# VectorE's copies of a finished sequence's small results: from the front of a sample step to behind the second half of its selected scores

## The chip, the cores and the metric

The program runs on one core of one Trainium2 chip. A core has a TensorE (PE, with its weight load PEld), a VectorE (DVE), a ScalarE (ACT), a GpSimd (POOL) and a SyncE (SP) that here only issues transfers. Every engine runs its own instructions in their order; where one needs another's result it waits on a semaphore, and everything behind the waiting instruction on that engine waits with it. The metric is the device time of one execution in microseconds, the median of several runs.

## The reference

One layer of a decoder, run for a prompt of 512 tokens and for 8 sample sequences that share all weights. The part that matters here is the sample side: each of the 8 sequences has one new token and 4096 past positions. Cut to that:

```python
# per sample sequence b; SCALE and masks left out
o_s = softmax(q . k_selected) @ v_selected     # 15 selected blocks of 64 rows + the new row
o_w = softmax(q . k_window)   @ v_window       # the last 512 rows + the new row
o_mem = softmax(mq . k_mem)   @ v_mem          # 256 memory rows, 4 heads
o_fox = softmax(fq . k_past + decay) @ v_past  # all 32 pages of 128 rows
# prompt and sample: three branches, silu gates, and a merge
z = branch * silu(gate) @ w_branch
y = x + rmsnorm(sum_k sigmoid(xn @ w_gate_k) * z_k @ w_out, g_post)
```

## The kernel before

The kernel runs five stages one after the other: compression of cached pages, norms, the input projection, the prompt's attention, and `sample_and_merge`. The change lies in the last. It interleaves two jobs. The merge of the prompt is heavy matmul work, cut by `Plan` into items: a product is two gate halves of 260 columns (line 1730, x16 in the trace for one half) and, from the thirteenth product on, a branch product z (line 1738, x8 in the trace for one). The 8 sample sequences are 8 steps `b` of a loop that every engine walks in its own written order, with merge items in slots 0 to 8 of each step (`merge_until(b, slot)`), one or two items a slot. The last 3 sequences' fox attention (32 pages each of keys and values) is spread over the steps too.

What each engine does around the change, in step `b`:

- **VectorE** (the list in the diff below): selected scores of group 0 (`small_scores(b, "slc", 0)`, lines 2051 and 2055), merge slot 0, one group of page scores (`page_scores`, lines 2064 and 2066), then `small_sums(b - 1)`: it copies the previous sequence's small sums out of PSUM (lines 2138 and 2139). Behind it come `query_diagonal("nsa", b + 1)` (line 2027, the diagonal from which TensorE spreads the next query), the selected scores of group 1, merge slot 1, `place_sums(b - 2)` (line 2146), `query_diagonal("mem", b + 1)`, the window scores, the query rows (line 2033), memory scores (lines 2074 and 2076), more merge and page scores, and the maxima of the softmax (line 2099).
- **TensorE**: merge slot 0, `small_values(b - 1)` (lines 1803 and 1806, the previous sequence's weighted sums into PSUM), merge slot 1, `turn_sums(b - 2)` (line 1815), `spread_query("nsa", b + 1)` (line 1749), merge slot 2, `spread_query("mem", b + 1)`, merge slots 3 and 4 with `page_values` between (line 1766, fox values), then `softmax_step(b, 0)` (line 1777), which needs the maxima.

`small_sums(b - 1)` waits for two things: `small_free`, that `small_values(b - 1)` is done, and `sums_turned`, that `turn_sums(b - 2)` has read the one buffer `svs` it writes. On TensorE the second lies behind merge slot 1. TensorE's order in a step:

```python
merge_until(b, 0)
small_values(b - 1)          # -> small_free
merge_until(b, 1)
turn_sums(b - 2)             # -> sums_turned
spread_query("nsa", b + 1)   # waits for VectorE's diagonal
merge_until(b, 2)
spread_query("mem", b + 1)   # waits for VectorE's second diagonal
```

SyncE issues the transfers of pages in a fixed order (keys and values alternating): a key load waits for VectorE's `k_free` (line 1640 on), a value load for TensorE's `v_free` (line 1655), and each stands in line behind the ones before. There are three value buffers of two pages each. ScalarE turns the gate halves out of PSUM (line 1953 on) and loads the next gate weights. GpSimd gathers the selected rows two sequences ahead (line 1714).

Of the kernel before, what the change touches and what calls it, by code (L numbers as in the profile page):

```python
# [79 lines left out]
def after(engine, s, count):  # L80

    if count > 0:
        engine.wait_ge(s, count)
# [1438 lines left out]
def sample_and_merge(k):  # L1522
# [11 lines left out]
    with ExitStack() as cx:  # L1534
# [101 lines left out]
        with nc.Block() as block:  # L1636
# [354 lines left out]
            def _(ve):  # L1991
# [5 lines left out]
                def merge_product(product):  # L1997
                    ve.wait_ge(g_out, 2 * product + 2)
                    if product < SILU:
                        nc.vector.tensor_tensor(k.oT[:, product, :], e[product % 2], k.oT[:, product, :], ALU.mult).then_inc(e_free, 1)  # L2000
                        return
                    n = product - SILU
                    d, b = n // 3, n % 3
                    ve.wait_ge(z_done, n + 1)
                    if b == 2:
                        ve.wait_ge(mt_done, 2 * d + 1)
                    elif b == 1:
                        after(ve, mt_done, 2 * d)
                    nc.vector.scalar_tensor_tensor(out=tmp if b else mt[:, d, :], in0=e[product % 2], scalar=1.0, in1=z_bank[:, :],
                                                   op0=ALU.add, op1=ALU.mult).then_inc(e_free, 1)  # L2010
                    if b:
                        ve.wait_ge(e_free, product + 1)
                        nc.vector.tensor_tensor(mt[:, d, :], mt[:, d, :], tmp, ALU.add).then_inc(mt_done, 1)

                def merge_until(b, slot):

                    for product in range(merged[0], Plan.products(Plan.until(b, slot))):
                        merge_product(product)
                    merged[0] = max(merged[0], Plan.products(Plan.until(b, slot)))
# [4 lines left out]
                def query_diagonal(kind, b):  # L2024
                    after(ve, q_spread, event[kind, b])
                    q, seq = (k.qf, fox_at[b]) if kind == "fox" else (k.mq if kind == "mem" else k.qn, b)
                    nc.vector.tensor_tensor(qdiag, k.ident.unsqueeze(1).to_broadcast([P, 4, P]),  # L2027
                                            q[:, seq, :].unsqueeze(2).to_broadcast([P, 4, P]), ALU.mult).then_inc(qdiag_done, 1)
# [6 lines left out]
                def small_scores(b, kind, g):  # L2035

                    n, ss = b * 4 + parts_of(b).index((kind, g)), ss_of[b % 2]
                    ve.wait_ge(q_in, event["nsa", b] + 1)
                    after(ve, small_free, b - 1)
                    if kind == "win":  # L2040
                        ve.wait_ge(win_in, (b + 1) * 16)
                    else:
                        ve.wait_ge(slc_in[b % 2], (b // 2 + 1) * 16 * NSLC)
                    after(ve, small_scored, n - 1)
                    tiles = NWIN if kind == "win" else 8
                    feats = slice(g * HD, (g + 1) * HD)
                    keys = win[:, :, feats] if kind == "win" else slc[:, b % 2, g * 8:g * 8 + 8, feats]
                    at = (n % 2) * 2048
                    product = scratch[:, at:at + R * tiles * HD].rearrange("p (r n d) -> p r n d", r=R, n=tiles)
                    rows = qrows_of["nsa"][:, g * R * HD:(g + 1) * R * HD].rearrange("p (r d) -> p r d", r=R)  # L2050
                    nc.vector.tensor_tensor(product, keys.unsqueeze(1).to_broadcast([P, R, tiles, HD]),  # L2051
                                            rows.unsqueeze(2).to_broadcast([P, R, tiles, HD]), ALU.mult).then_inc(small_times, 1)
                    ve.wait_ge(small_times, n + 1)
                    first = ST if kind == "win" else 0
                    nc.vector.tensor_reduce(ss[:, first:first + tiles, g * R:(g + 1) * R].rearrange("p n r -> p r n"), product,  # L2055
                                            AX, ALU.add).then_inc(small_scored, 1)

                def page_scores(m):
                    b, g = EARLY + m // GROUPS, m % GROUPS
                    ve.wait_ge(k_in[m % KG], 16 * KR * (m // KG + 1))  # L2060
                    if g == 0:
                        ve.wait_ge(q_in, event["fox", first_step(b)] + 1)
                    pages = kpage[:, (m % KG) * KR:(m % KG + 1) * KR, :]
                    nc.vector.tensor_tensor(pages, pages, qrow[:, 0, :].unsqueeze(1).to_broadcast([P, KR, BRW]), ALU.mult).then_inc(k_times, 1)  # L2064
                    ve.wait_ge(k_times, m + 1)
                    nc.vector.tensor_reduce(k.pfe[:, b - EARLY, g * KR:(g + 1) * KR, :], pages.rearrange("p n (h d) -> p n h d", h=H),  # L2066
                                            AX, ALU.add).then_inc(k_free, 1)
# [67 lines left out]
                def small_sums(b):  # L2135
                    ve.wait_ge(small_free, b + 1)
                    after(ve, sums_turned, b)
                    nc.vector.tensor_copy(svs, sv_bank.rearrange("p (i n) -> p i n", i=2)).then_inc(os_out, 1)
                    nc.vector.tensor_copy(k.om[:, :, b:b + 1], om_turned.unsqueeze(2)).then_inc(os_out, 1)
# [42 lines left out]
                for b in range(NB):  # L2182
                    late = list(groups_of(b))
                    if b:
                        small_scores(b, "slc", 0)
                    merge_until(b, 0)
                    for m in late[0:1]:
                        page_scores(m)
                    if b:
                        small_sums(b - 1)  # L2190
                    if b < LASTB:
                        query_diagonal("nsa", b + 1)
                    if b:
                        small_scores(b, "slc", 1)
                    merge_until(b, 1)
                    if b > 1:
                        place_sums(b - 2)
                    if b - 1 in sums_after:
                        place_fox(sums_after[b - 1])
                    if b < LASTB:  # L2200
                        query_diagonal("mem", b + 1)
                    small_scores(b, "win", 0)
                    small_scores(b, "win", 1)
                    if b and b < LASTB:
                        query_row("nsa", b + 1)
                    merge_until(b, 2)
                    memory_scores(b)
                    if b and b < LASTB:
                        query_row("mem", b + 1)
                    merge_until(b, 3)  # L2210
                    for m in late[1:2]:
                        page_scores(m)
                    if b == 0:
                        small_scores(b, "slc", 0)
                        merge_until(b, 4)
                        small_scores(b, "slc", 1)
                        query_row("nsa", b + 1)
                        query_row("mem", b + 1)
                    merge_until(b, 4)
                    scores(b)  # L2220
                    softmax_max(b)
                    for m in late[2:3]:
                        page_scores(m)
                    merge_until(b, 5)
                    softmax_spread(b)
                    for m in late[3:4]:
                        page_scores(m)
                    if b + 1 in fox_at:
                        query_diagonal("fox", b + 1)
                    softmax_shift(b)  # L2230
                    merge_until(b, 6)
                    softmax_sum(b)
                    merge_until(b, 7)
                    softmax_norm(b)
                    if b + 1 in fox_at:
                        query_row("fox", b + 1)
                    if b in sums_after:
                        page_sums(sums_after[b])
                    if b in fox_of:
                        probabilities()  # L2240
                    merge_until(b, 8)
# [188 lines left out]
```

## Time and profile before

| what | value |
|---|---|
| median of 3 runs | 1405.1 us (1399.25 to 1415.84) |
| profiled execution | 1402.47 us, its span 1400.7 us |
| PE busy, share of the span | 1231.3 us, 88% |
| DVE busy, share of the span | 804.9 us, 57% |
| ACT, POOL busy | 229.1 us, 176.3 us |
| sample stage: first query to last `small_values` | 801 to 1316 us of the span |

The stage of interest is the last 600 us. Steps 1 to 7 begin on TensorE near 897, 952, 1013, 1074, 1136, 1199 and 1253 us (the `small_values` of the sequence before), and the eighth `small_values` is at 1312 us. In the timeline a row gives start, duration, engine, line, operation, tiles and shape, and in brackets the engine's idle time before it and what ended that. "cst" at line 2027 is the diagonal, and `d_ybuf` at line 2138 is the buffer `svs`. `score_banks` and `bank` are PSUM.

### The profile page before, as it was taken

To read this page: it belongs to the slowest core of one execution; us is meant where nothing else is said; L and a number is where in the kernel's file an instruction comes from. 1 tells how busy PE (TensorE), PEld (TensorE's weight loads), DVE (VectorE), ACT (ScalarE), POOL (GpSimd) and SP (SyncE) were. 2 spreads that over 40 slices of the span, in tenths; PEclk is the share of its full clock that TensorE was granted. 3 is DMA by queue.
4 is the path that set the end of the run, shared out by engine and by line. 5 is a ranking of instruction groups with operands and counts; after the bars stand their busy time and mean duration, and the time that the engine had idled before them with its cause. 6 is when DMAs were issued, how large, how long until landed. Compare 5 with 4: busy or idle time off the path is not lost. (4 is left out here: it accounts for less than half of the span.)

```text
span 1400.7 us, 23870 instructions
## 1 busy us (share of the span) xinstructions
PE 1231.3 (88%) x8308; PEld 841.1 (60%) x8308; DVE 804.9 (57%) x1168; ACT 229.1 (16%) x694; POOL 176.3 (13%) x150
## 2 busy tenths in 40 slices
PE   0889969999999569999999797988799898999996
PEld 0889958887888355444434476866556464665542
DVE  3445240798999862344544547577875868634123
ACT  0100141112111202233333400110000000000023
POOL 1010000200000000000000172244051331400000
PEclk9998989999999665999999988999999999999998
DMA  8899632577888502575876194566577776757620
GB/s 243 236 284 264 203 117 64 165 232 247 285 295 306 138 1 76 181 271 181 272 248 225 40 299 143 163 183 220 157 246 243 237 264 211 235 176 272 248 84 31
DMA packets 238846, 279.65 MB, mean 200 GB/s; under 512 B 21685, under 2 KB 159438, under 8 KB 238470
## 3 DMA queue, kind: packets, MB, share of 16 engines
q1 hardware_dynamic: 126534, 200.28, 42.9%
q10 hardware_dynamic: 105760, 60.01, 15.4%
q0 software_dynamic: 6432, 17.83, 3.9%
q8 instruction: 66, 1.08, 0.3%
q14 instruction: 54, 0.44, 0.1%
HBM read 271.13 MB, written 11.11 MB: 201 GB/s over the span
## 5 line engine op out<-in xcount | busy, mean ns | idle before, releaser
L1730 PE MATMUL bank<-xnT,e_wg 128*128 128x260 f32 x1152 | 280.1, 402 | 0.0
L1730 PEld LDWEIGHTS bank<-xnT,e_wg 128*128 128x128 f32 x1152 | 228.7, 201 | 53.4 <-issue 16.2
L580 PE MATMUL score_banks<-xnT,oT 128*128 128x260 f32 (+1 forms) x864 | 197.9, 387 | 7.5 <-DMA oT<-in_w_in 7.5
L1714 POOL DMA_INDIRECT d_slc<-in_cache_nsa_slc,selrow x128 | 153.6, 1200 | 274.6 <-PE score_banks L1806 235.2
L580 PEld LDWEIGHTS score_banks<-xnT,oT 128*128 128x128 f32 (+1 forms) x864 | 162.1, 190 | 37.8 <-DMA oT<-in_w_in 7.8
L253 PE MATMUL score_banks<-c_cols,c_w 128*64 128x128 f32 (+2 forms) x2304 | 121.3, 269 | 46.7 <-DVE c_cols L293 46.5
L253 PEld LDWEIGHTS score_banks<-c_cols,c_w 128*64 128x64 f32 x2304 | 119.5, 141 | 47.4 <-issue 47.1
L293 DVE COPY c_cols<-oT 128x1024 f32<-128x1024 f32 x48 | 49.8, 1163 | 87.1 <-DMA oT<-in_cache_nsa_cmp 80.4
L1393 DVE TENSOR_REDUCE f_pt<-score_banks 128x2 f32<-128x512 f32 (+3 forms) x56 | 45.1, 805 | 80.5 <-PE score_banks L1314 78.4
L1738 PE MATMUL bank<-oT,e_wb 128*128 128x512 f32 x192 | 90.7, 617 | 0.0
L1358 PE MATMUL bank<-mt,rpast 128*8 128x512 f32 x320 | 61.9, 610 | 8.5 <-DMA mt<-in_cache_fox_kv 7.4
L1411 DVE COPY f_pt<-bank 128x128 f32<-128x128 f32 (+2 forms) x68 | 27.6, 421 | 66.2 <-PE bank L1325 66.0
L1738 PEld LDWEIGHTS bank<-oT,e_wb 128*128 128x128 f32 x192 | 36.8, 197 | 42.8 <-issue 42.2
L1953 ACT ACTIVATE cst<-bank 128x260 f32<-128x260 f32 x36 | 14.0, 388 | 285.9 <-PE bank L1730 285.9
L2055 DVE TENSOR_REDUCE d_ss<-d_kpage 128x16 f32<-128x1024 f32 (+1 forms) x32 | 56.2, 1755 | 1.1
L2066 DVE TENSOR_REDUCE rpast<-d_kpage 128x32 f32<-128x2048 f32 x24 | 54.9, 2286 | 0.8
L2064 DVE TENSOR_TENSOR d_kpage<-d_kpage,d_qrow 128x2048 f32<-128x2048 f32 x24 | 54.8, 2282 | 0.3 <-DMA d_kpage<-in_cache_fox_kv 0.3
L1440 ACT ACTIVATE mnT<-score_banks,f_pt 128x256 f32<-128x256 f32 (+3 forms) x76 | 38.8, 515 | 80.0 <-DVE f_pt L1393 79.7
L742 DVE TENSOR_REDUCE sfe<-mt 128x16 f32<-128x1024 f32 x40 | 48.8, 1220 | 1.4
L742 DVE TENSOR_REDUCE sfe<-oT 128x16 f32<-128x1024 f32 x40 | 48.8, 1220 | 1.4
L740 DVE TENSOR_TENSOR mt<-mt,p_qrow 128x1024 f32<-128x1024 f32 x40 | 48.9, 1223 | 1.1 <-DMA mt<-in_cache_fox_kv 1.1
L740 DVE TENSOR_TENSOR oT<-oT,p_qrow 128x1024 f32<-128x1024 f32 x40 | 49.0, 1225 | 0.5 <-DMA oT<-in_cache_fox_kv 0.5
(392 smaller groups left out, 1449.0 us busy)
## 6 DMA issues: line engine op xcount, KB each, us to landing
mt<-in_cache_fox_kv SPq DMA_DIRECT2D x240, 256.0 KB, 3.9
d_kpage<-in_cache_fox_kv SPq DMA_DIRECT2D x96, 256.0 KB, 4.7
d_vpage<-in_cache_fox_kv SPq DMA_DIRECT2D x96, 256.0 KB, 4.0
oT<-in_cache_fox_kv SPq DMA_DIRECT2D x80, 256.0 KB, 3.8
e_wg<-in_w_in ACTq DMA_DIRECT2D x36, 512.0 KB, 5.2
oT<-in_cache_nsa_cmp SPq DMA_DIRECT2D x128, 128.0 KB, 3.7
oT<-in_w_in ACTq DMA_DIRECT2D x13, 1024.0 KB, 7.3
oT<-in_cache_nsa_cmp ACTq DMA_DIRECT2D x64, 128.0 KB
```

Source lines behind the costliest of these rows:

```text
L253: last = nc.tensor.matmul(hp[s][halves[v], 0:n], w1[:, v, d, :], cols[s][:, d, 0:n], start=d == 0, stop=d == HD - 1)
L293: nc.vector.tensor_copy(dst, src).then_inc(page_free[slot], 1)
L580: last = nc.tensor.matmul(pj[ch.n % 2][i][0:ch.w, 0:NM if ch.mem else TH], w[:, c, ch.off:ch.off + ch.w], rhs, start=c == 0, stop=c == DC - 1)
L740: nc.vector.tensor_tensor(slot, slot, qrow[b % 2][:, :].unsqueeze(1).to_broadcast([P, KR, BRW]), ALU.mult).then_inc(k_times, 1)
L742: nc.vector.tensor_reduce(k.sfe[:, b, g * KR:(g + 1) * KR, :], slot.rearrange("p n (h d) -> p n h d", h=H), AX, ALU.add).then_inc(k_free, 1)
L1358: last = nc.tensor.matmul(fv_bank[32 * i:32 * i + H, :], k.pfe[:, b, page, :], vpage[:, (n % VG) * KV + i % KV, :], start=g == 0, stop=g = ...
L1714: nc.gpsimd.indirect_dma_start(out=slc[:, b % 2, n, :], out_offset=None, in_=k.cache_slc, in_offset=bass.IndirectOffsetOnAxis(ap=k.selrow[ ...
L1730: last = nc.tensor.matmul(gate_bank[n % 2][:, 0:TH], wg[product % WR][:, c, :], k.xnT[:, c, part * TH:(part + 1) * TH], start=c == 0, stop ...
L1738: last = nc.tensor.matmul(z_bank[:, :], wb[n % 2][:, c, :], k.oT[:, (n % 3) * 4 + c, :], start=c == 0, stop=c == 3)
L2055: nc.vector.tensor_reduce(ss[:, first:first + tiles, g * R:(g + 1) * R].rearrange("p n r -> p r n"), product, AX, ALU.add).then_inc(small_ ...
L2064: nc.vector.tensor_tensor(pages, pages, qrow[:, 0, :].unsqueeze(1).to_broadcast([P, KR, BRW]), ALU.mult).then_inc(k_times, 1)
L2066: nc.vector.tensor_reduce(k.pfe[:, b - EARLY, g * KR:(g + 1) * KR, :], pages.rearrange("p n (h d) -> p n h d", h=H), AX, ALU.add).then_inc ...
```

## The change

In every step from 1 on, VectorE's `small_sums(b - 1)` stands behind `merge_until(b, 1)` instead of ahead of `query_diagonal("nsa", b + 1)`. No instruction is added or removed, and no other engine's order changes.

```diff
                     merge_until(b, 0)
                     for m in late[0:1]:
                         page_scores(m)
-                    if b:
-                        small_sums(b - 1)
                     if b < LASTB:
                         query_diagonal("nsa", b + 1)
                     if b:
                         small_scores(b, "slc", 1)
                     merge_until(b, 1)
+                    if b:
+                        small_sums(b - 1)
                     if b > 1:
                         place_sums(b - 2)
```

VectorE's order in step 2 before the change; line 2066 ends the page scores, 2138 and 2139 are the copies, 2027 the diagonals, 2051 and 2055 the selected scores, 2009 and 2013 merge slot 1:

```order
L2066 TENSOR_REDUCE rpast<-d_kpage 128x32
L2138 COPY d_ybuf<-score_banks 128x256
L2139 COPY om<-score_banks 128x4
L2027 TENSOR_TENSOR cst<-cst,qn 128x512
L2051 TENSOR_TENSOR d_kpage<-d_slc,d_ybuf 128x2048
L2055 TENSOR_REDUCE d_ss<-d_kpage 128x4x8
L2009 SCALAR_TENSOR_TENSOR cst<-cst,bank 128x512
L2013 TENSOR_TENSOR mt<-mt,cst 128x512
L2146 COPY ow<-score_banks 64x2x4 x2
L2027 TENSOR_TENSOR cst<-cst,mq 128x512
```

The same place after the change:

```order
L2066 TENSOR_REDUCE rpast<-d_kpage 128x32
L2027 TENSOR_TENSOR cst<-cst,qn 128x512
L2051 TENSOR_TENSOR d_kpage<-d_slc,d_ybuf 128x2048
L2055 TENSOR_REDUCE d_ss<-d_kpage 128x4x8
L2009 SCALAR_TENSOR_TENSOR cst<-cst,bank 128x512
L2013 TENSOR_TENSOR mt<-mt,cst 128x512
L2138 COPY d_ybuf<-score_banks 128x256
L2139 COPY om<-score_banks 128x4
L2146 COPY ow<-score_banks 64x2x4 x2
L2027 TENSOR_TENSOR cst<-cst,mq 128x512
```

The two copies went behind five instructions: the nsa diagonal, the two of the selected scores and the two of the merge.

In step 3 no merge product falls into slot 1 on VectorE, so the difference there is three instructions long:

```order
 L2066 TENSOR_REDUCE rpast<-d_kpage 128x32
+L2027 TENSOR_TENSOR cst<-cst,qn 128x512
+L2051 TENSOR_TENSOR d_kpage<-d_slc,d_ybuf 128x2048
+L2055 TENSOR_REDUCE d_ss<-d_kpage 128x4x8
 L2138 COPY d_ybuf<-score_banks 128x256
 L2139 COPY om<-score_banks 128x4
-L2027 TENSOR_TENSOR cst<-cst,qn 128x512
-L2051 TENSOR_TENSOR d_kpage<-d_slc,d_ybuf 128x2048
-L2055 TENSOR_REDUCE d_ss<-d_kpage 128x4x8
 L2146 COPY ow<-score_banks 64x2x4 x2
 L2027 TENSOR_TENSOR cst<-cst,mq 128x512
```

There the copies went behind the diagonal and the selected scores, and the second diagonal follows them at once.

## Rows read from the trace of the kernel before

**Rows 1.** Waits from 895 to 1318 us: engine, line, releaser: total us, times, longest.
```profile
DVE d_ybuf L2138 <- PE score_banks L1815: 61.5, 7, 19.6
...
PEld bank L1766 <- DMA d_vpage<-in_cache_fox_kv: 14.8, 13, 3.3
```

**Rows 2.** Timeline of VectorE in step 2: start us, us, operation, idle before.
```profile
965.52 0.42 DVE L2138 COPY d_ybuf<-score_banks 128x256 f32<-128x256 f32 x1 [5.92 <-PE score_banks L1815]
...
965.93 0.68 DVE L2027 TENSOR_TENSOR cst<-cst,qn 128x512 f32<-128x512 f32 x1
...
971.12 0.68 DVE L2009 SCALAR_TENSOR_TENSOR cst<-cst,bank 128x512 f32<-128x512 f32 x1
...
972.82 0.69 DVE L2027 TENSOR_TENSOR cst<-cst,mq 128x512 f32<-128x512 f32 x1
```

**Rows 3.** Timeline of TensorE in step 2.
```profile
961.48 3.60 PE L1738 MATMUL bank<-oT,e_wb 128*128 128x512 f32 x8
964.91 0.51 PE L1815 MATMUL score_banks<-cst,d_ybuf 128*128 128x4 f32 x4
966.67 1.12 PE L1749 MATMUL score_banks<-cst 128*128 128x512 f32 x2 [1.25 <-DVE cst L2027]
...
973.57 1.13 PE L1749 MATMUL score_banks<-cst 128*128 128x512 f32 x2 [2.26 <-DVE cst L2027]
...
988.95 0.39 PE L1777 MATMUL score_banks<-cst,d_mx 128*28 128x128 f32 x1 [7.31 <-DVE d_mx L2099]
```

**Rows 4.** Timelines of VectorE and TensorE in step 1.
```profile
910.09 0.69 DVE L2000 TENSOR_TENSOR oT<-cst,oT 128x512 f32<-128x512 f32 x1 [1.87 <-ACT cst L1956]
...
925.71 0.39 PE L1777 MATMUL score_banks<-cst,d_mx 128*20 128x128 f32 x1 [3.90 <-DVE d_mx L2099]
```

**Rows 5.** Waits of TensorE from 1013 to 1253 us (steps 3 to 6).
```profile
PE score_banks L1749 <- DVE cst L2027: 11.0, 8, 2.6
PE bank L1766 <- DMA d_vpage<-in_cache_fox_kv: 5.0, 5, 2.3
PE score_banks L1777 <- DVE d_mx L2099: 3.8, 2, 3.3
```

**Rows 6.** Timeline of VectorE in steps 3 and 4.
```profile
1026.16 0.42 DVE L2138 COPY d_ybuf<-score_banks 128x256 f32<-128x256 f32 x1 [7.02 <-PE score_banks L1815]
...
1032.07 0.69 DVE L2027 TENSOR_TENSOR cst<-cst,mq 128x512 f32<-128x512 f32 x1
...
1086.82 0.42 DVE L2138 COPY d_ybuf<-score_banks 128x256 f32<-128x256 f32 x1 [8.43 <-PE score_banks L1815]
...
1093.33 0.69 DVE L2027 TENSOR_TENSOR cst<-cst,mq 128x512 f32<-128x512 f32 x1
```

**Rows 7.** Timeline of TensorE in steps 3 and 4.
```profile
1055.90 1.03 PE L1766 MATMUL bank<-d_vpage,d_pf 128*8 128x512 f32 x4 [1.36 <-DMA d_vpage<-in_cache_fox_kv]
1057.24 1.03 PE L1766 MATMUL bank<-d_vpage,d_pf 128*8 128x512 f32 x4 [0.31 <-DMA d_vpage<-in_cache_fox_kv]
...
1110.15 0.39 PE L1777 MATMUL score_banks<-cst,d_mx 128*28 128x128 f32 x1 [3.27 <-DVE d_mx L2099]
```

**Rows 8.** Timelines of VectorE and of SyncE's queue in step 3.
```profile
1044.12 2.29 DVE L2066 TENSOR_REDUCE rpast<-d_kpage 128x32 f32<-128x2048 f32 x1
...
1051.42 1.92 SPq L1655 DMA_DIRECT2D d_vpage<-in_cache_fox_kv  x4
```

**Rows 9.** Page's issues (KB each, us to landing); chain of waits in step 5.
```profile
d_vpage<-in_cache_fox_kv SPq DMA_DIRECT2D x96, 256.0 KB, 4.0
...
1167.77 7.52 DMA d_vpage<-in_cache_fox_kv
```

**Rows 10.** Busy time by stretch: us, engines, granted clock PEclk, DMA share, GB/s.
```profile
989.00:999.00 10.00, 10.00 (x36) 8.11 (x37) 9.53 (x8) 0.84 (x3) 0.00 (x0) 0.78 0.58 189
...
1077.00:1083.00 6.00, 6.00 (x16) 2.93 (x16) 1.39 (x1) 0.00 (x0) 3.66 (x4) 0.72 0.76 217
```

**Rows 11.** Timeline of TensorE in step 4, behind `small_values`.
```profile
1077.49 5.38 PE L1738 MATMUL bank<-oT,e_wb 128*128 128x512 f32 x8
```

## The prediction

> **What bounds the kernel now.** I read the waits over the eight sample steps first, then the timelines of VectorE and TensorE side by side in one step, then the waits of TensorE step by step, and last the rows of the transfers. TensorE is the engine that the end waits for (88% of the span in the table). So a change on VectorE is worth only what TensorE waits for VectorE, and what it waits for transfers that VectorE releases.
>
> The waits show VectorE idle for 61.5 us in seven places ahead of one instruction, the first copy of `small_sums`, always until `turn_sums` on line 1815 is done [rows 1]. Step 2 shows what that does. VectorE stands idle for 5.92 us, copies, and only then makes the diagonal [rows 2]. TensorE, which has just let it go, now waits 1.25 us for that diagonal, 2.26 us for the second one, and 7.31 us for the softmax maxima, which come at the end of VectorE's whole list [rows 3]. The engines wait for each other in turn. In steps 3 to 6 TensorE waits 11.0 us for eight diagonals, 3.8 us for two maxima and 5.0 us for value pages [rows 5].
>
> **The change, part by part.** Nothing is added. Seven pairs of copies move, each 965.93 - 965.52 = 0.41 us from its start to the next instruction [rows 2]. What counts is who stands behind them.
>
> *Step 2, worked through.* VectorE's idle time began at 965.52 - 5.92 = 959.60. The diagonal and the selected scores take 971.12 - 965.93 = 5.19 us, the merge with `place_sums` 972.82 - 971.12 = 1.70 us [rows 2]. In the new order the diagonal and the scores run from 959.60 to 964.79. The merge needs z, which ends at 961.48 + 3.60 = 965.08 [rows 3], so it starts near 965.2. With 1.70 for merge and placing and 0.41 for the copies, the second diagonal starts at 967.3 instead of 972.82: VectorE is 5.5 us ahead. The copies come at about 966.5, when `turn_sums` has ended (964.91 + 0.51 = 965.42 [rows 3]), so they wait for nothing. TensorE finds the first diagonal ready and saves 1.25. It would come to the second at 973.57 - 2.26 - 1.25 = 970.1; that diagonal is ready at 967.3 + 0.7 = 968.0, so 2.26 go too. TensorE is 3.5 us ahead, VectorE 5.5. At the maxima TensorE used to arrive at 988.95 - 7.31 = 981.6; it now arrives at 978.1, the maxima let it go at 988.95 - 5.5 = 983.4, and 5.3 us of waiting stay. The step gains VectorE's lead, **5.5 us**.
>
> *Step 1.* Here VectorE did not wait at the copies: a 1.87 us wait for ScalarE follows behind the scores and absorbs them [rows 4]. Behind that wait the copies have no cover, so VectorE's list gets 0.41 longer up to the maxima, for which TensorE waits 3.90 us already [rows 4]. I take a **loss of 0.5 us**, between nothing (if ScalarE's result comes sooner) and one pair of copies with its hand-over.
>
> *Steps 3 to 6.* In step 3 the copies stay where they are in time, at 1026.16, since `turn_sums` still lets them go, but the diagonal and the scores now lie in the 7.02 us of idle time ahead of them [rows 6]. Behind them come only `place_sums` and the second diagonal, which needs the first spread (1.12 us [rows 3]): it starts at about 1027.2 instead of 1032.07 [rows 6], 4.9 us ahead. In step 4 the same working gives 1087.8 instead of 1093.33, 5.5 us ahead [rows 6]. TensorE's longest wait for a diagonal was 2.6 us [rows 5], so all eight go: **11.0 us**, 2.75 a step in the mean. Of the 3.8 us at maxima [rows 5] step 4 had 3.27 [rows 7]; there VectorE gains 5.5 - 2.75 = 2.75 on TensorE, so 0.5 stays and **3.3 us** go.
>
> *Value pages.* In step 3 TensorE waits 1.36 + 0.31 = 1.7 us for two pairs of pages [rows 7]. These loads stand in SyncE's queue behind a key load that waits for VectorE's page scores, which end at 1044.12 + 2.29 = 1046.4; the value loads go out from 1051.42 [rows 8]. They move with VectorE (4.9), while TensorE comes 2.75 + 0.5 sooner: the **1.7 us** go. The other 3.3 of the 5.0 I leave in place. In step 5 the pair with the long wait goes out at 1167.77, in TensorE's own time (a buffer must come free), and takes 7.52 us against a median of 4.0 [rows 9]. This I bound from both sides: 3.3 us more if those pages also come sooner, and a loss for pages that don't, a rival below.
>
> *Step 7.* VectorE's longest idle time, 19.6 us [rows 1], is here, but no next query is spread and its maxima were in time: nothing.
>
> What becomes late: the copied sums are next read by `turn_sums(b - 1)` a whole step later, some 60 us on TensorE, so that some us more hurt nobody. SyncE, ScalarE and GpSimd keep their orders.
>
> Sum: 5.5 - 0.5 + 11.0 + 3.3 + 1.7 = **21.0 us**. The profiled execution took 1402.5 us, so 1381.5. The median of the runs is 1405.1, 2.6 higher, with runs from 1399 to 1416, so the level itself is good to some us only.
>
> **The clock.** Behind TensorE's wait of 7.31 us in step 2 the next 10 us show a granted clock of 0.78 in the mean, a mix of the two levels 1.2 and 2.4 GHz [rows 10]. I let this stay, since most of that wait stays. Behind the small matmuls of `small_values` the clock falls as well: 0.72 in step 4 [rows 10], where one z takes 5.38 us [rows 11] against 3.60 [rows 3], a loss of 1.8. Six of the seven steps show one like it (by step 4, an estimate of 10.8 us together). I leave them in, because the work around `small_values` is not changed. The Trainium skill (TensorE: Matmul & The Clock Gate, Part 1: The HAM clock gate) says that "the default state is throttled, and activity releases the throttle": by that rule fewer waits would also mean fewer falls, and the time would come out lower than my sum, as in the third rival. The trace agrees as far as the fall behind the 7.31 us goes; whether the shorter waits ahead of `small_values` have a part in the others it does not show.
>
> **The rivals.**
> 1. *Only the diagonals gain.* VectorE spends its lead before the maxima, at a query row or a merge product that needs TensorE. Then TensorE gains 3.5 in step 2 and 11.0 in steps 3 to 6, less 0.5: 14 us, **1388.5**. For it: VectorE has such waits all through a step. Against: in step 2's timeline VectorE is never idle between the second diagonal and the maxima.
> 2. *The pages take the gain back.* Value pages come when they came before, because the transfers and not the releases set their time. What steps 3 to 5 gain (2.75 + 0.5 + 1.7, then 5.5, then 2.75, together 13.2) is then waited off on line 1766. 21.0 - 13.2 = 7.8 is left: **1394.7**. For it: TensorE or its weight load already met late pages 13 times [rows 1]. Against: median landing of 4.0 us, with the release of the step 3 pages traced to VectorE [rows 8, 9].
> 3. *The clock gains too.* The six falls behind `small_values` vanish: 10.8 more, **1370.7**.
> 4. *Slower: late pages.* Denser steps push key, value, gather and weight loads into each other, and a pair of value pages costs 7.52 instead of 4.0 us, 3.5 more, with TensorE waiting for it. Six such pairs undo the 21 us; from ten of the 48 on it is slower by over 1%. Twelve give 42 us: 1402.5 - 21 + 42 = **1423.5**. For it: one such pair exists. Against: of 14.8 us lost on the weight load at pages in all 48 pairs [rows 1] no wait passed 3.3.
>
> That the wait does not go at all is no case of its own: part of it does stay at the copies (steps 3, 4, 6 and 7), but with the first diagonal and the scores no longer behind it.
>
> **How the numbers follow.** The forecast has 0.55, rival 1 0.12, rival 2 0.14, rival 3 0.14, rival 4 0.05. A measurement of this kernel can tell about 1%, 14 us, from no change; that is 1388.5 on the profiled level, the edge on which rival 1 sits. Faster by over 1%: 0.55 + 0.14 + half of 0.12 = 0.75. Within 1%: 0.14 + 0.06 = 0.20. Slower: 0.05. The range goes from rival 3 with a little below it (1369) to rival 2 with a little above it (1396); outside lie rival 4 and the far ends of 2 and 3. The forecast's own range is 1376 to 1387: 3.3 us of pages and the 2.6 between profile and median on either side.
>
> **What would show it.** In the profile after: the idle time ahead of line 2138 falls from 61.5 us to about 23 (some 2 in steps 3 and 4 each, 5 in step 6, 14 of the 19.6 in step 7); TensorE's waits on line 1749 in steps 2 to 6 fall from 14.5 us to about nothing; the wait on line 1777 in step 2 falls from 7.3 to about 5.3 and in step 4 from 3.3 to under 1; waits on line 1766 stay at 3 to 4 us. I am wrong if line 1749 still waits, if line 1766 waits over 10 us, or if the steps lose at another line what they gain at 1749.

## The result, and the profile after

The changed kernel takes 1385.3 us (median of 4 runs, 1381.9 to 1389.9) against 1402.2 us beside it: a ratio of 0.987, interval 0.982 to 0.992. Measured twice more, the same kernel gave 0.990 (0.986 to 0.994) and 0.987 (0.984 to 0.991). By these ratios it is faster by 14 to 18 us, a little over 1%, where 21 us were forecast. The profiled execution took 1389.9 us, the longest of the four; its span is 1388.2.

The waits of TensorE between the first and the last `small_values` (893 to 1300 us), engine, line, releaser: total us, times, longest:

```profile
PE bank L1766 <- DMA d_vpage<-in_cache_fox_kv: 10.7, 7, 3.9
PE score_banks L1777 <- DVE d_mx L2099: 6.9, 2, 4.4
PE score_banks L1780 <- DVE d_dia L2106: 2.3, 2, 1.3
PE bank L1738 <- DMA e_wb<-in_w_branch: 2.3, 1, 2.3
PE score_banks L1749 <- DVE cst L2027: 1.0, 1, 1.0
```

and VectorE's at the copies:

```profile
DVE d_ybuf L2138 <- PE score_banks L1815: 16.0, 4, 8.1
```

The waits for diagonals (line 1749) are gone but for one of 1.0 us in step 1, which stood there before as well. Value pages now head the list. Before, they were 5.0 us [rows 5].

Step 2 on VectorE after, as [rows 2]: start us, us, operation, and in brackets the idle time before it.

```profile
956.10 0.68 DVE L2027 TENSOR_TENSOR cst<-cst,qn 128x512 f32<-128x512 f32 x1
...
961.76 0.69 DVE L2009 SCALAR_TENSOR_TENSOR cst<-cst,bank 128x512 f32<-128x512 f32 x1 [0.45 <-PE bank L1738]
...
963.09 0.42 DVE L2138 COPY d_ybuf<-score_banks 128x256 f32<-128x256 f32 x1
...
963.87 0.69 DVE L2027 TENSOR_TENSOR cst<-cst,mq 128x512 f32<-128x512 f32 x1
```

The diagonal and the scores start at once, the merge waits 0.45 us for z, and the copies wait for nothing. The same step on TensorE, as [rows 3]:

```profile
961.86 1.10 PE L1749 MATMUL score_banks<-cst 128*128 128x512 f32 x2
...
966.31 1.02 PE L1749 MATMUL score_banks<-cst 128*128 128x512 f32 x2
...
973.13 5.40 PE L1738 MATMUL bank<-oT,e_wb 128*128 128x512 f32 x8 [2.29 <-DMA e_wb<-in_w_branch]
981.11 0.39 PE L1777 MATMUL score_banks<-cst,d_mx 128*28 128x128 f32 x1 [2.59 <-DVE d_mx L2099]
```

Both spreads run without a wait. Of the 7.31 us at the maxima 2.59 stay, and ahead of that TensorE now waits 2.29 us for a branch weight that it used to find loaded.

Steps 4 and 5 on TensorE, where the value pages are:

```profile
1087.92 1.03 PE L1766 MATMUL bank<-d_vpage,d_pf 128*8 128x512 f32 x4 [2.14 <-DMA d_vpage<-in_cache_fox_kv]
...
1101.87 1.03 PE L1766 MATMUL bank<-d_vpage,d_pf 128*8 128x512 f32 x4 [1.08 <-DMA d_vpage<-in_cache_fox_kv]
1104.56 1.88 PE L1766 MATMUL bank<-d_vpage,d_pf 128*8 128x512 f32 x4 [1.66 <-DMA d_vpage<-in_cache_fox_kv]
...
1106.92 9.20 PE L1730 MATMUL bank<-xnT,e_wg 128*128 128x260 f32 x32
...
1159.80 1.88 PE L1766 MATMUL bank<-d_vpage,d_pf 128*8 128x512 f32 x4 [3.94 <-DMA d_vpage<-in_cache_fox_kv]
...
1161.80 8.99 PE L1730 MATMUL bank<-xnT,e_wg 128*128 128x260 f32 x32
```

The same places in the kernel before:

```profile
1120.41 1.03 PE L1766 MATMUL bank<-d_vpage,d_pf 128*8 128x512 f32 x4 [0.73 <-DMA d_vpage<-in_cache_fox_kv]
...
1121.70 7.28 PE L1730 MATMUL bank<-xnT,e_wg 128*128 128x260 f32 x32
...
1175.33 1.03 PE L1766 MATMUL bank<-d_vpage,d_pf 128*8 128x512 f32 x4 [2.32 <-DMA d_vpage<-in_cache_fox_kv]
...
1176.41 7.18 PE L1730 MATMUL bank<-xnT,e_wg 128*128 128x260 f32 x32
```

The 0.7 us at pages of step 4 have become 4.9, and the pair in step 5 that cost 2.3 costs 3.9. Here the clock follows. These are the stretches behind the last two waits (us, PE, PEld, DVE, ACT, POOL busy, granted clock, DMA share, GB/s):

```profile
1106.90:1116.00 9.10, 9.10 (x35) 7.61 (x34) 2.04 (x9) 0.98 (x4) 0.00 (x0) 0.78 0.72 250
1161.80:1170.70 8.90, 8.90 (x33) 7.17 (x32) 4.99 (x4) 0.39 (x1) 0.00 (x0) 0.79 0.31 100
```

In the kernel before, the same two gate items ran at 1.00 and took 7.28 and 7.18 us, so the falls cost 1.9 and 1.8 us on top.

Step 6 has no page wait, and its two waits for diagonals are gone, but it is no shorter. There the clock fell behind `small_values`, where it had not fallen before. The gate item behind it, before and after:

```profile
1202.85 7.26 PE L1730 MATMUL bank<-xnT,e_wg 128*128 128x260 f32 x32
...
1190.69 9.96 PE L1730 MATMUL bank<-xnT,e_wg 128*128 128x260 f32 x32
```

The granted clock over the whole step is 1.00 before and 0.94 after.

The length of each step, from one `small_values` on TensorE to the next, is the clearest account (us, worked out from the starts of line 1803 in each timeline):

| step | before | after | second profile | third | gain in the first | forecast |
|---|---|---|---|---|---|---|
| 1 | 55.6 | 55.7 | 55.6 | 55.5 | -0.1 | -0.5 |
| 2 | 60.5 | 55.6 | 55.4 | 54.7 | 4.9 | 5.5 |
| 3 | 60.7 | 57.3 | 58.2 | 57.0 | 3.4 | 4.95 |
| 4 | 62.3 | 61.3 | 60.3 | 56.2 | 1.0 | 5.5 |
| 5 | 63.0 | 63.1 | 61.0 | 62.3 | -0.1 | 2.75 |
| 6 | 54.1 | 54.2 | 54.7 | 54.0 | -0.1 | 2.75 |
| 7 | 59.1 | 59.3 | 57.3 | 58.7 | -0.2 | 0 |
| sum | 415.4 | 406.4 | 402.4 | 398.5 | 9.0 | 21 |

Steps 1 to 3 did about what was worked out. Steps 4 to 6 gave back what they had gained, in the first profile nearly all of it, in the others part. The rest of the 12.5 us between the two spans lies ahead of step 1, where nothing changed (3.5 us); in the fourteen profiles of this document step 1 begins anywhere from 887 to 901 us.

Waits and longer matmuls can be told apart. Over the seven steps TensorE waited 37.8 us before, and 23.2, 25.1 and 22.0 us in the three profiles after: 12.7 to 15.8 us less. For the same matmuls it was busy 377.4 us before, and 383.1, 377.1 and 376.4 us after. So the first profile lost 5.7 us of its 14.6 to longer matmuls, and the other two lost none; in its steps 4 to 6 the granted clock was 0.92, 0.92 and 0.94, against 0.95, 0.97 and 1.00 before.

### The profile page after: what moved, and what is told of

Same layout as the page of the kernel before. It is cut to its first block and busy times, and to the rows that moved or that the text cites. A ratio compares the mean times of both kernels' runs of the same rounds, so it can differ in the third digit from the quotient of the medians.

```text
span 1388.2 us, 23870 instructions
## 1 busy us (share of the span) xinstructions
PE 1231.0 (89%) x8308; PEld 841.4 (61%) x8308; DVE 805.8 (58%) x1168; ACT 228.9 (16%) x694; POOL 181.8 (13%) x150
## 3 DMA queue, kind: packets, MB, share of 16 engines
q8 instruction: 66, 1.08, 0.3%
## 5 line engine op out<-in xcount | busy, mean ns | idle before, releaser
L1714 POOL DMA_INDIRECT d_slc<-in_cache_nsa_slc,selrow x128 | 159.1, 1243 | 256.3 <-PE score_banks L1806 216.9
L1358 PE MATMUL bank<-mt,rpast 128*8 128x512 f32 x320 | 60.5, 609 | 6.9 <-DMA mt<-in_cache_fox_kv 5.8
L1411 DVE COPY f_pt<-bank 128x128 f32<-128x128 f32 (+2 forms) x68 | 27.6, 421 | 61.3 <-PE bank L1325 61.1
L2064 DVE TENSOR_TENSOR d_kpage<-d_kpage,d_qrow 128x2048 f32<-128x2048 f32 x24 | 54.7, 2281 | 3.9 <-DMA d_kpage<-in_cache_fox_kv 3.9
L2055 DVE TENSOR_REDUCE d_ss<-d_kpage 128x16 f32<-128x1024 f32 (+1 forms) x32 | 56.2, 1755 | 1.1
```

The costliest lines, as they stand in the source:

```text
L1358: last = nc.tensor.matmul(fv_bank[32 * i:32 * i + H, :], k.pfe[:, b, page, :], vpage[:, (n % VG) * KV + i % KV, :], start=g == 0, stop=g = ...
L1714: nc.gpsimd.indirect_dma_start(out=slc[:, b % 2, n, :], out_offset=None, in_=k.cache_slc, in_offset=bass.IndirectOffsetOnAxis(ap=k.selrow[ ...
```

## The experiments

Theory A is the forecast's sum. Theory B, and P for its main part, is that late value pages (and the clock behind them) take back what steps 4 to 6 gain. The numbers in brackets behind a ratio are its 95% interval.

**The changed kernel again, twice.** No edit.

> The changed kernel once more, nothing else changed, for a tighter ratio and a second profile. Theory A (the forecast's sum: steps 2 to 6 gain 21 us together, and the profile of the first execution was a poor draw): ratio 0.985 to 0.988, and steps 4 to 6 of the second profile are 1 to 5 us shorter each than before. Theory B (late value pages and the clock take back what steps 4 to 6 gain, in every execution): ratio near 0.993, steps 4 to 6 as long as before within 1 us each.

> The changed kernel beside the three runs with four page buffers, on one chip. Both theories: 1385 to 1389 us, TensorE waits 10 to 13 us for value pages.

Ratios 0.990 and 0.987, TensorE's waits for value pages 12.8 and 8.8 us:

```profile
PE bank L1766 <- DMA d_vpage<-in_cache_fox_kv: 12.8, 7, 3.4
```

The steps are in the table. They lie between A and B: step 5 is never over 2 us shorter, step 4 between 1 and 6. So the first profile was no odd draw as to the page waits (8.8 is a little below the 10 to 13 expected), but the amount lost varies by execution. Step 4 shows how much of that is the clock: it waits 4.9 us for pages in the first profile and 4.5 in the third, yet it is 61.3 us long in the one, at a granted clock of 0.92, and 56.2 in the other, at 1.00.

**Only the first diagonal ahead of the copies.** Shown against the kernel before.

```diff
+                    if b < LASTB:
+                        query_diagonal("nsa", b + 1)
                     if b:
                         small_sums(b - 1)
-                    if b < LASTB:
-                        query_diagonal("nsa", b + 1)
                     if b:
                         small_scores(b, "slc", 1)
                     merge_until(b, 1)
```

> The copies move behind the first diagonal only; the selected scores stay behind the copies. If the gain comes from VectorE's whole list standing behind the copies (theory A), the first spread finds its diagonal ready (1.25 us in each of steps 2 to 6), but VectorE's list is only 0.6 us sooner, so the waits for the second diagonal and the maxima grow by what the first one saved: 3 us in all, ratio 0.998. If only the first diagonal mattered (rival), 1.25 us x 5 = 6.3 us, ratio 0.9955, with the wait for the second diagonal unchanged.

1397.9 us, ratio 0.9965 (0.993 to 0.9997): 5 us of gain, between the two numbers, and the interval holds both. TensorE's waits from 880 to 1320 us say more:

```profile
PE score_banks L1749 <- DVE cst L2027: 13.4, 6, 3.4
PE score_banks L1777 <- DVE d_mx L2099: 12.6, 3, 5.6
```

Six waits for diagonals are left of eleven, but they still make 13.4 us: most of each first wait that went came back at the second diagonal, up to 3.4 us where 2.6 was the longest. In sum 28.3 us with line 1780, against 32.8 before. In this profile the seven steps are no shorter (415.8 us against 415.4), since TensorE was busy 4.7 us longer for the same matmuls. With the scores and the merge left behind the copies only 2.1 of the 15.5 us at diagonals go; with them ahead of the copies 14.5 go.

**Late copies in steps 1 to 3, or in steps 4 to 7.** Two kernels, shown against the kernel before; each asks for the new place in its own steps and for the old one elsewhere.

```diff
-                    if b:
+                    if b and not (b <= 3):   # the other kernel: not (b >= 4)
                         small_sums(b - 1)
...
+                    if b and (b <= 3):       # the other kernel: (b >= 4)
+                        small_sums(b - 1)
```

> The copies stand late in steps 1 to 3 only, as before in steps 4 to 7. Theory A: -0.5 + 5.5 + 4.95 = 10 us of gain, ratio 0.993. Theory B: 8.3 us (what these steps show between the two profiles), ratio 0.994. Both close; with the run of the late steps beside it the two gains add up to the whole or they don't.

> The copies stand late in steps 4 to 7 only, as before in steps 1 to 3. Theory A: 5.5 + 2.75 + 2.75 = 11 us of gain, ratio 0.992. Theory B (pages and the clock take it back): 1 us, ratio 0.999.

Steps 1 to 3: 1398.4 us, ratio 0.997 (0.994 to 1.001), 4 us where 8 to 10 were expected; the interval reaches 9, so it leaves room for B's 8.3 but not for A's 10. Steps 4 to 7: 1394.7 us, ratio 0.995 (0.992 to 0.998), 7 us (3 to 11) where A said 11 and B said 1. So B in its sharp form falls: the late steps do gain, by the time about two thirds of their sum; in the profile steps 4 to 7 are 3.1 us shorter. The two gains together, 11 us, are less than the whole change's 14 to 18, but their intervals are too wide to tell. In the second kernel TensorE waits for pages:

```profile
PE bank L1766 <- DMA d_vpage<-in_cache_fox_kv: 10.5, 6, 3.6
```

Step 3, with the old place, has 1.7 of them; the other 8.8 us are those of steps 4 and 5, as in the whole change. The profiled execution of the first kernel took 1410.0 us, 12 above its median, and is not used here; what came back behind step 3 is not shown.

**Value pages of a quarter of the bytes, old order and new.** The same loads, for the first 128 of 512 columns, so part of the fox values of the last three sequences is left out. The other columns are set to zero once ahead of the loads (not shown).

```diff
-                    sp.dma_start(vpage[:, (m % VG) * VR + i % VR, :].unsqueeze(1),
-                                 k.cache_fox[bass.ds(pg, 1), :, 1, :].rearrange("a p n -> p a n")).then_inc(v_in[m % VG], 16)
+                    sp.dma_start(vpage[:, (m % VG) * VR + i % VR, 0:P].unsqueeze(1),
+                                 k.cache_fox[bass.ds(pg, 1), :, 1, 0:P].rearrange("a p n -> p a n")).then_inc(v_in[m % VG], 16)
```

> The kernel before with value pages of a quarter of the bytes (the first 128 of 512 columns of each page are loaded, the rest is zero, so the fox values of the last three sequences are left out in part). TensorE, VectorE and ScalarE do the same instructions. Both theories: the 5 us that TensorE waits for value pages go, and time is about 1397.

> The changed kernel with value pages of a quarter of the bytes (the same part of the fox values is left out). If late value pages are what takes back the forecast's missing 4 to 7 us (theory P), the 11 to 13 us that TensorE waits for pages in the changed kernel go, time is about 1376, and the gain over the run with the same loads and the old order is 20 us (the forecast's 21 less its 1.7 of pages). If the clock or something else takes it back (rival), the gain over that run stays at 13 to 15 us and time is about 1383.

1396.5 and 1377.7 us: the change is worth 18.7 us there, beside 13.7 to 20.1 with whole pages (16.9 at first), and the changed kernel comes out 8 to 11 us below its own whole-page runs. TensorE's waits in the new order:

```profile
PE score_banks L1779 <- DVE d_mx L2101: 11.1, 3, 5.7
PE bank L1768 <- DMA d_vpage<-in_cache_fox_kv: 3.8, 6, 1.4
```

Page waits fell to 3.8 us, and part of what they gave moved to the maxima (11.1 instead of 6.9, both lines two further down in this file). In the old order no page wait is left, and the ratio to the kernel before is 0.995 (0.992 to 0.998), 7 us, which agrees with the 5 expected. The 18.7 us are near A less its page term (19.3), but with an interval of about 11 to 26 they cannot be told from the gain with whole pages. The steps say more: from 409.9 to 387.4 us, 22.5 less, where whole pages gave 9.0, 13.0 and 16.9. P holds in its direction: with pages out of the way the steps gain what the waits on VectorE had made them lose.

The waits do not hold the whole price of a late page. Over the seven steps the 192 page matmuls of line 1766 (1768 in this file) are busy 39.0 us in the kernel before and 38.0 to 40.4 with the change, but 30.8 and 33.7 us here. A late page also holds up the weight load of its matmul (14.8 us before [rows 1], 1.7 and 9.0 here), and the longer page matmuls go with it. The change itself does not alter this share.

**SyncE's order turned.**

```diff
-                    for which in "kvvkvkvkvvvvv":
+                    for which in "kvvvkkvkvvvvv":
```

> The changed kernel, with SyncE's order of page loads in a step turned from key, value, value, key, value, key, value, key to key, value, value, value, key, key, value, key: the values for slot 5 no longer stand behind a key load that waits for VectorE's page scores. Theory P: TensorE's waits for the pages of slot 5 (1.5 to 2.1 us in step 3, 2.7 to 3.4 us in step 4 of the two profiles) go, time 4 us below the changed kernel, about 1383 to 1385. Rival: the key load that now stands behind comes late for the page scores of slot 5, VectorE waits for it and nothing is gained or 2 to 4 us are lost.

1387.5 us, ratio 0.987 (0.982 to 0.991): no difference to the change alone can be told, nor can P's 4 us be ruled out. The pages fell to 6.0 us, but VectorE now waits for key pages (880 to 1320 us):

```profile
DVE d_kpage L2064 <- DMA d_kpage<-in_cache_fox_kv: 10.4, 3, 4.1
```

and with it TensorE at new places (1.9 us at the denominators, 2.8 at a diagonal). The page waits of step 3 are gone, those of step 5 stay at 3.3. By the waits the rival was right for this edit alone.

**One group of page scores behind the maxima, steps 0 to 2.**

```diff
-                    for m in late[1:2]:
+                    for m in late[1:2] if b > 2 else ():
                         page_scores(m)
...
                     softmax_max(b)
-                    for m in late[2:3]:
+                    for m in late[1:3] if b <= 2 else late[2:3]:
                         page_scores(m)
```

> The changed kernel, with one group of page scores (4.6 us) moved behind the softmax maxima in steps 0 to 2. What the forecast left at the maxima is a wait for VectorE's list: 6.9, 4.4 and 2.6 us in steps 0 to 2. If VectorE's length up to there sets it, they fall to 2.3, 0 and 0 us, the wait for the spread maxima behind it (line 1780) grows by 1 to 2 us a step, and 6 us are gained: about 1382. Rival: the page scores are then late everywhere behind, and the waits on line 1780 and line 1783 take all of it back: no change.

1388.0 us, ratio 0.985 (0.979 to 0.991): nothing beyond the change that can be told. The waits moved one line on (880 to 1320 us, so without step 0):

```profile
PE score_banks L1780 <- DVE d_dia L2106: 6.0, 3, 2.9
PE score_banks L1783 <- DVE d_den L2116: 4.4, 1, 4.4
PE score_banks L1777 <- DVE d_mx L2099: 2.9, 2, 2.6
```

6.9 us at the maxima became 2.9 (in step 0, 6.9 became 4.3), but 2.3 on line 1780 became 6.0 and line 1783 took 4.4. Step 1 got 3.1 us shorter and step 2 4.7 longer. In steps 1 and 2 this other order of the same list only chose where TensorE waits.

**Four value buffers.** With three, a value load waits until TensorE has freed one. Room came from tiles that are idle by then (three small ones of the last stretch too, not shown); no instruction changes.

```diff
-    KG, VG, VR = 2, 3, 2
+    KG, VG, VR = 2, 4, 2
...
-        fvs = sb("d_fvs", [P, BRW])
+        fvs = k.rpast[:, 3 * PAGES:EARLY * PAGES, :].rearrange("p n h -> p (n h)")
```

> The changed kernel with four value-page buffers instead of three (the fox copy buffer and three small tail tiles lie in memory that is idle by then; no instruction differs). Theory P, part one (a value load waits until TensorE has freed one of three buffers): the waits in step 5 (3.0 to 3.9 us) and in slot 3 of step 4 (1.8 to 2.1 us) go, and with them the fall of the clock behind the first; those in slot 5 of steps 3 and 4 stay, since their loads stand behind a key load. 5 to 7 us below the changed kernel: 1380 to 1383. Rival (the transfers themselves are late, not their issue): the same waits at the same places, no gain.

> Four value-page buffers and SyncE's order with the values for slot 5 ahead of the key load. Theory P, both parts: nearly all page waits go (under 3 us stay), 8 to 11 us below the changed kernel: 1376 to 1380, close to what quarter-size pages gave. Rival: VectorE's waits for late key pages (10 us in the run with the turned order alone) become waits of TensorE for maxima or denominators: no better than four buffers alone.

> The kernel before with four value-page buffers. TensorE waited 5.0 us for pages there, and VectorE's late diagonals hid most of the lateness: 3 to 5 us below the kernel before (about 1398), so the change is worth more with four buffers (16 to 18 us) than with three (14). Rival: no difference to the kernel before.

On one chip: the change alone 1385.4, with four buffers 1379.8 (0.981, 0.978 to 0.985), with four buffers and the turned order 1370.5 (0.976, 0.972 to 0.979), the old place with four buffers 1395.5 (0.992, 0.989 to 0.995). With four buffers step 5 is 55.8 us long (62.3 in the run of the change beside it), but 7.8 us of page waits stay. With the turned order too they are gone (880 to 1320 us, lines one further down in this file):

```profile
PE score_banks L1778 <- DVE d_mx L2100: 10.6, 4, 4.3
PE bank L1739 <- DMA e_wb<-in_w_branch: 3.9, 1, 3.9
PE score_banks L1781 <- DVE d_dia L2107: 3.4, 3, 1.3
PE score_banks L1750 <- DVE cst L2028: 2.4, 2, 1.4
PE bank L1767 <- DMA d_vpage<-in_cache_fox_kv: 0.4, 1, 0.4
```

VectorE's waits for keys fell as well:

```profile
DVE d_kpage L2065 <- DMA d_kpage<-in_cache_fox_kv: 4.5, 2, 2.6
```

Steps 3 to 6 are 55.8, 58.1, 53.9 and 52.8 us long, 20 us less than before in these four. The seven steps take 387.8 us against 398.5 for the change beside it. Both parts of P are shown, with whole pages: the issue was late, by a missing buffer in step 5 and by SyncE's queue in steps 3 and 4, and only together do the two edits pay in full. Of the 10.7 us that the seven steps are shorter only 1.3 are waits in sum, since TensorE then waits more for VectorE; the page matmuls are busy 30.2 us instead of 40.4. This version beats both kernels, by 35 us and by 15. With four buffers the change is worth 15.6 us, and the turned order takes off another 9.3; the turned order in the old place was not run. Two numbers came out better than expected: the old place gained 7 to 15 us by four buffers where 3 to 5 were expected, and the two edits together came 6 us below their 1376 to 1380. The page matmuls, which the expectations left out, go the same way: 31.2 us in the old place with four buffers, against 39.0 before.

## Why the prediction was right, and where its sum was too large

The 21.0 us were a sum of TensorE's waits, and of these 14.6, 12.7 and 15.8 us went in the three profiles. The first rival's 1388.5 lies as near the measured times as the forecast does, but its mechanism did not come: the lead did reach the maxima, as steps 2 and 4 show.

**VectorE's idle time is refilled, and the diagonals come in time: right.** The eight waits of steps 3 to 6 (11.0 us) and the two of step 2 (3.5 us) [rows 3, 5] are all gone. Step 2's second diagonal was worked out to come 7.7 us behind the first idle moment (967.3 - 959.6) and came 963.87 - 956.10 = 7.8 behind it.

**Step 2 gains VectorE's lead, 5.5: right (4.9).** TensorE still waits about 5 us ahead of the maxima, but 2.29 of them for a branch weight. That wait lies in front of one for VectorE, where TensorE would have stood anyway.

**Step 1 loses 0.5: right in kind.** Its maxima came with a wait of 4.4 us instead of 3.90 [rows 4]. The step did not get longer, since the fall of the clock behind `small_values` is missing in it this time (granted clock from 1.5 to 12.5 us behind its start: 0.84 before, 1.00 after).

**Copies: the order of size was right.** 16.0 us of idle time, some 1.9 and 2.7 in steps 3 and 4, 8.1 in step 6, 3.3 in step 7. The forecast put 14 into step 7; there VectorE now waits for z ahead of the copies instead.

**Value pages: the wrong term.** "The other 3.3 of the 5.0 I leave in place", and the 1.7 of step 3 would go. Measured are 8.8 to 12.8 us in all, and 1.5 stayed in step 3. The prediction's own sign of being wrong, over 10 us of waits on line 1766, came in two of three profiles (10.7 and 12.8; 8.8 in the third). VectorE's release came 5 us sooner there, as said. But the transfer of the second pair took 5.51 us instead of 4.19, and TensorE had moved too. In steps 4 and 5 rows of the chain of waits show the pairs that came last:

```profile
1097.92 6.59 DMA d_vpage<-in_cache_fox_kv
...
1150.64 9.12 DMA d_vpage<-in_cache_fox_kv
```

SyncE put the first of them behind a key load:

```profile
1092.52 2.25 SPq L1646 DMA_DIRECT2D d_kpage<-in_cache_fox_kv  x4
1096.34 1.92 SPq L1655 DMA_DIRECT2D d_vpage<-in_cache_fox_kv  x4
```

and the second left when TensorE freed a buffer. So TensorE got ahead of pages whose issue hung on SyncE's queue in step 4 and on its own progress in step 5, and its lead turned into a wait for them. That is the second rival's place with a part of its price: not all of 13.2 us, but 5.5 to 9.5, which leaves 11.5 to 15.5 of the 21. The longer matmuls of the first profile (5.7 us) come on top of that. The forecast weighed the pages as a case of all or nothing. What was missing is a count of the round trip: buffer freed, load issued, 6 to 9 us of transfer, against the time until TensorE needs it.

**The clock.** The rival in which the falls vanish did not come. The fall behind `small_values` in step 4 reads the same (5.38 us for one z, the very value of [rows 11]). The one behind the maxima of step 4 is gone with its wait, two new ones stand behind page waits, and one behind `small_values` in step 6. The forecast had no term for falls that differ between executions of one kernel. At the pages of step 4 the third profile waits at the same place and does not fall:

```profile
1097.04 1.03 PE L1766 MATMUL bank<-d_vpage,d_pf 128*8 128x512 f32 x4 [0.46 <-DMA d_vpage<-in_cache_fox_kv]
1100.02 1.03 PE L1766 MATMUL bank<-d_vpage,d_pf 128*8 128x512 f32 x4 [1.96 <-DMA d_vpage<-in_cache_fox_kv]
...
1101.31 7.28 PE L1730 MATMUL bank<-xnT,e_wg 128*128 128x260 f32 x32
```

The Trainium skill has it (TensorE: Matmul & The Clock Gate, Part 1: The HAM clock gate) that "the default state is throttled, and activity releases the throttle". By that rule a wait costs more than its length. The trace agrees in step 5 of the first profile, where 3.94 us of waiting was followed by 1.8 us of slower matmuls, but 2.4 us of waiting in the third profile was followed by none.

## What to carry to other kernels

A small copy that waits for another engine is dear by what stands behind it in its own engine's list: look for work there that needs nothing from the wait, and put it ahead. What the bounding engine then gains is only kept as far as its transfers can follow; where its own progress frees their buffers, count the round trip of the load before booking the gain, and look at the queue in which it stands. The list of waits does not hold all that a late load costs: see whether the matmuls that read it get shorter when it is on time. When a removed wait comes back at a transfer, both the number of buffers and the issue order may have to move: here either alone gave 0 to 6 us, the two together 15.

## What the runs showed of the hardware

A 256 KB value page landed in 4.0 us in the median [rows 9], but in 6.6 and 9.1 us in stretches where the transfer engines were busy 0.93 and all of the time (1.01 by the profile). With pages on time or nearly so, the same 192 page matmuls were busy 30 to 31 us instead of 38 to 40, so a late page cost more than the 5 to 13 us that TensorE is seen to wait for it. TensorE's granted clock fell to a mean of 0.78 (a mix of its two levels, 1.2 and 2.4 GHz) behind waits of 1.08 and 1.66 us with one short group of page matmuls between them; behind waits of 0.46 and 1.96 us at the same place, in another execution of the same kernel, the gate item took the 7.28 us that it takes without a fall. So which wait is followed by a fall cannot be read from the waits alone here.
